# A float32 two-block network on one core: high and low parts of the feed-forward input side by side, as one moving operand of 512 columns

## What is computed

```
def swiglu(x, w1, w2):
    gu = x @ w1
    g, u = gu[..., :D_FF], gu[..., D_FF:]
    return (jax.nn.silu(g) * u) @ w2

for l in range(DEPTH):                                    # block 1, DEPTH = 2
    x = x + 0.5 * swiglu(rms_norm(x, ffn1_norm[l]), ffn1_w1[l], ffn1_w2[l])
    x = x + hybrid_mixer(rms_norm(x, mix_norm[l]), ...)
    x = x + 0.5 * swiglu(rms_norm(x, ffn2_norm[l]), ffn2_w1[l], ffn2_w2[l])
return rms_norm(x, final_norm)
```

## Time and profile before

| what | value |
|---|---|
| median of 3 runs | 2327.35 us (2321.9 to 2327.54) |
| profiled execution | 2319.62 us |
| its span, first to last instruction | 2317.8 us |
| mean granted TensorE clock in it | 0.931 of full |
| busy share of the span | TensorE 88%, its weight loads 84%, VectorE 64%, ScalarE 50%, GpSimd 6% |
| matmuls | 15496, each with a weight load |
| read from HBM | 327.27 MB |

### The profile page before, as it was taken

One profiled execution on the slowest core, in us unless ns is written; L12 is line 12 of the kernel. 1 busy time (PEld: TensorE's weight loads), 2 busy tenths in 40 slices (PEclk: granted clock), 3 DMA queues, 4 the chain that ended last, 5 costly groups with the idle time before them and its releaser, 6 DMA issues.

```text
span 2317.8 us, 40039 instructions
## 1 busy us (share of the span) xinstructions
PE 2045.6 (88%) x15496; PEld 1951.3 (84%) x15496; DVE 1472.7 (64%) x2084; ACT 1168.3 (50%) x1804; POOL 149.5 (6%) x167
## 2 busy tenths in 40 slices
PE   6999877879999999878879998787899978887998
PEld 6999867879999999867879998665799976667998
DVE  5665698655655655698656655564598465626963
ACT  5445644444444445644444445554565445536753
POOL 0071000000000001000000001000300000003000
PEclk9999989989999999989989999887899988878999
DMA  5545323345545545323345454331254532202543
GB/s 206 182 167 184 128 100 109 118 165 173 178 163 191 184 162 184 128 100 110 123 161 180 170 170 156 109 109 37 73 197 157 190 125 98 103 19 106 210 147 118
DMA packets 53535, 329.83 MB, mean 142 GB/s; under 512 B 5936, under 2 KB 6704, under 8 KB 27952
## 3 DMA queue, kind: packets, MB, share of 16 engines
q1 hardware_dynamic: 53424, 328.34, 41.0%
HBM read 327.27 MB, written 1.05 MB: 142 GB/s over the span
## 4 chain that ended last, share of the span: by engine, by line
PE 49%; DVE 16%; ACT 12%; issue 10%; DVEq 7%; DMA 3%; POOLq 3%; POOL 1%; ACTq 0%; SPq 0%
PE bank L605 13%; PE bank L606 13%; PE bank L607 13%; DVE w_lo L584 7%; ACT w_hi L578 5%; DMA raw<-in_w 2%; DVEq L915 2%; DVE conv L1239 2%; DVEq L1233 2%; PE bank L617 1%; ACT probs L924 1%; PE bank L626 1%; PE bank L619 1%; PE bank L1522 1%; PE bank L1538 1%
## 5 line engine op out<-in xcount | busy, mean ns | idle before, releaser
L584 DVE TENSOR_TENSOR w_lo<-raw,w_hi 128x2048 fp32r<-128x2048 f32 (+3 forms) x358 | 719.2, 2010 | 433.1 <-ACT w_hi L578 430.6
L605 PE MATMUL bank<-h_hi,w_hi 128*128 128x256 f32 x2704 | 784.9, 290 | 17.7 <-DVE w_lo L584 16.4
L606 PE MATMUL bank<-h_lo,w_hi 128*128 128x256 f32 x2704 | 775.7, 287 | 0.0
L607 PE MATMUL bank<-h_hi,w_lo 128*128 128x256 f32 x2704 | 774.9, 287 | 0.0
L578 ACT ACTIVATE w_hi<-raw 128x2048 fp32r<-128x2048 f32 (+3 forms) x358 | 600.9, 1680 | 170.7 <-DMA raw<-in_w 118.3
L605 PEld LDWEIGHTS bank<-h_hi,w_hi 128*128 128x128 f32 x2704 | 531.2, 196 | 23.2 <-DVE w_lo L584 17.5
L606 PEld LDWEIGHTS bank<-h_lo,w_hi 128*128 128x128 f32 x2704 | 531.0, 196 | 1.0
L607 PEld LDWEIGHTS bank<-h_hi,w_lo 128*128 128x128 f32 x2704 | 529.9, 196 | 0.0
L605 PE MATMUL bank<-hid_hi,w_hi 128*128 128x256 f32 x1056 | 296.2, 281 | 6.5 <-DVE conv L1879 6.5
L606 PE MATMUL bank<-hid_lo,w_hi 128*128 128x256 f32 x1056 | 296.2, 280 | 0.0
L607 PE MATMUL bank<-hid_hi,w_lo 128*128 128x256 f32 x1056 | 296.1, 280 | 0.0
(11 more groups left out here) (356 smaller groups left out, 3275.2 us busy)
## 6 DMA issues: line engine op xcount, KB each, us to landing
raw<-in_w SPq DMA_DIRECT2D x198, 1024.0 KB, 4.8
raw<-in_w SPq DMA_DIRECT2D x96, 704.0 KB, 4.0
raw<-in_w SPq DMA_DIRECT2D x52, 768.0 KB, 4.2
raw<-in_w SPq DMA_DIRECT2D x8, 512.0 KB, 3.5
raw<-in_w SPq DMA_DIRECT2D x4, 576.0 KB, 3.9
x<-in_x SPq DMA_DIRECT2D x1, 1024.0 KB, 4.7
out<-x SPq DMA_DIRECT2D x4, 256.0 KB, 2.4
const<-in_const SPq DMA_DIRECT2D x1, 548.0 KB, 5.2
```

The costliest lines, as they stand in the source:

```text
L584: dve.tensor_tensor(w_lo[:, s % SPLIT_SLOTS, 0:n], raw[:, s % RAW_SLOTS, 0:n], w_hi[:, s % SPLIT_SLOTS, 0:n].bitcast(F32), ALU.subtract).t ...
L605: pe.matmul(out, hi, x_hi, start=start, stop=False)
L606: pe.matmul(out, hi, x_lo, start=False, stop=False)
L607: return pe.matmul(out, lo, x_hi, start=False, stop=stop)
```

## The change

In block 1's feed-forwards, from up unit 4 on and in all down tiles, the high and the low part of the activation become one moving operand of 512 columns. They now lie side by side for each tile (`h_pair`, `hid_pair`; the old names are views of them). The high weights stream both parts in one matmul: high x high lands in columns 0 to 255 of a bank, high weight x low activation in columns 256 to 511. The low weights still stream the high part alone, into columns 0 to 255. A product is then two matmuls instead of three, and its result is the sum of the two halves of a bank.

An up unit therefore takes two banks, one for the gate and one for the linear columns: banks 4 and 5 or 6 and 7 by the parity of j. TensorE waits for the release of unit j-2 instead of j-4. The halves are added when PSUM is emptied: ScalarE copies the second half of each bank to SBUF (`joint`, two tiles of `scr`), VectorE adds the first halves to it in two instructions, drains, and scales the sum. For a down tile VectorE adds the second half to x, drains, and adds the first. Units 0 to 3, the mixers and block 2 keep three matmuls for a product.

```
+PAIRS_FROM = 4
@@ Groups
             if kind.startswith("up"):
                 main, bank = i % 4, i % 4
+                if pairs and i >= PAIRS_FROM:
+                    bank = 4 + 2 * (i % 2)
@@ build
-        h_hi = sbuf("h_hi", [P, KT, T], F32R)
-        h_lo = sbuf("h_lo", [P, KT, T], F32R)
+        h_pair = sbuf("h_pair", [P, KT, 2, T], F32R)
+        h_hi, h_lo = h_pair[:, :, 0], h_pair[:, :, 1]
+        joint = scr[:, 4:8].rearrange("p (a b) t -> p a (b t)", a=2)
-            hid_hi = sbuf("hid_hi", [P, FT, T], F32R, phase)
-            hid_lo = sbuf("hid_lo", [P, FT, T], F32R, phase)
+            hid_pair = sbuf("hid_pair", [P, FT, 2, T], F32R, phase)
+            hid_hi, hid_lo = hid_pair[:, :, 0], hid_pair[:, :, 1]
+        def pair_product(pe, bank, s, block, pair, start, stop):
+            hi = w_hi[:, s % SPLIT_SLOTS, block * P:block * P + P]
+            lo = w_lo[:, s % SPLIT_SLOTS, block * P:block * P + P]
+            pe.matmul(bank[:, 0:2 * T], hi, pair.rearrange("p a t -> p (a t)"), start=start, stop=False)
+            return pe.matmul(bank[:, 0:T], lo, pair[:, 0], start=False, stop=stop)
@@ ffn_pe
+            def paired_unit(j, more):
+                s = at + j
+                weights_ready(pe, s, more)
+                for half in range(2):
+                    for k in range(KT):
+                        last = pair_product(pe, banks[4 + 2 * (j % 2) + half], s, half * KT + k, h_pair[:, k], k == 0, k == KT - 1)
+                last.then_inc(work.done_sem.sem, 1)
...
+                work.wait_banks_free(pe, l, [(up, 4), (up, 5)])
+                with pe.Fori(0, 4) as it:
+                    for u in range(4, 8):
+                        pe.wait_ge(*work.taken(l, (up, 0), it * 4 + (u - 2)))
+                        paired_unit(u, it * 4)
...
+                            if paired:
+                                last = pair_product(pe, banks[2 + g], s, b, hid_pair[:, k], k == 0, k == FT - 1)
@@ ffn_act, gated
+                if j >= PAIRS_FROM:
+                    act.wait_ge(*work.done(l, (up, 0), more + j))
+                    for half in range(2):
+                        last = act.activation(joint[:, parity, half * T:half * T + T], banks[4 + 2 * parity + half][:, T:2 * T], ACT.Copy)
+                    last.then_inc(second_out.sem, 1)
@@ ffn_dve, gated
+                else:
+                    dve.wait_ge(*second_out(l, more + (w * (FT - PAIRS_FROM) + j + 1 - PAIRS_FROM)))
+                    for half in range(2):
+                        part = joint[:, parity, half * T:half * T + T]
+                        dve.tensor_tensor(part, part, banks[4 + 2 * parity + half][:, 0:T], ALU.add)
+                    dve.drain()
+                    dve.tensor_tensor(halves(scaled[:, parity]), halves(joint[:, parity]), by_r(2),
+                                      ALU.mult).then_inc(work.freed["v"].sem, 1)
@@ ffn_dve, residual
                 dve.wait_ge(*work.done(l, (down, 0), more * 2 + 2 * t))
+                dve.scalar_tensor_tensor(x[:, more + t], banks[2 + t % 2][:, T:2 * T], 0.5, x[:, more + t], ALU.mult, ALU.add)
+                dve.drain()
                 dve.scalar_tensor_tensor(x[:, more + t], banks[2 + t % 2][:, 0:T], 0.5, x[:, more + t], ALU.mult,
                                          ALU.add).then_inc(work.freed["v"].sem, 1)
```

More of the change, by code:

```diff
@@ L153, in __init__ @@
             self.mark[g], self.bank[g] = marks, bank
-            self.before[g] = last.get(bank)
+            taken = (bank, bank + 1) if pairs and kind.startswith("up") and i >= PAIRS_FROM else (bank,)
+            self.before[g] = [(b, last.get(b)) for b in taken]
             if who is None:
@@ L158, in __init__ @@
             self.freer[g] = (who, self.freed_until[who])
-            last[bank] = g
+            for b in taken:
+                last[b] = g
         self.marks, self.last = marks, last
@@ L418, in bank_free @@
             def bank_free(self, layer, group):
[L420 removed]
+                (bank, before), = self.g.before[group]
                 wrapped = before is None
[L422 to L423 removed]
+                who, n = self.g.freer[before or self.g.last[bank]]
                 s = self.freed[who]
@@ L433, in wait_banks_free @@
                     latest[who] = max(latest.get(who, n), n)
-                for group in groups:
-                    before = self.g.before[group]
+                for bank, before in (b for group in groups for b in self.g.before[group]):
                     wrapped = before is None
-                    who, n = self.g.freer[before or self.g.last[self.g.bank[group]]]
+                    who, n = self.g.freer[before or self.g.last[bank]]
                     latest[who] = max(latest.get(who, -10 ** 9), n - (self.freed[who].per if wrapped else 0))
@@ L763, in ffn_pe @@
                 by_tiles(pe, work, l, [((up, 3), at + 3)], lambda k: nm.true_ready(l, k + 1))
+                first = 4
+            else:
+                first_products(pe, nm, work, l, m, [((up, j), at + j) for j in range(2)], lambda: norm_pe(pe, work, nm, l, n))
+                first = 2
+            if paired:
+                for j in range(first, 4):
+                    up_unit(j, 0)
+                work.wait_banks_free(pe, l, [(up, 4), (up, 5)])
[3 more added lines that the diff above has]
+                        paired_unit(u, it * 4)
+                for j in range(20, FT):
+                    pe.wait_ge(*work.taken(l, (up, j - 2)))
+                    paired_unit(j, 0)
+            else:
+                for j in range(first, 4):
+                    up_unit(j, 0)
                 with pe.Fori(0, 4) as it:
@@ L770, in ffn_pe @@
                     up_unit(j, 0)
-            else:
-                first_products(pe, nm, work, l, m, [((up, j), at + j) for j in range(2)], lambda: norm_pe(pe, work, nm, l, n))
-                with pe.Fori(0, 5) as it:
-                    for u in range(4):
-                        pe.wait_ge(*work.taken(l, (up, 0), it * 4 + (2 + u - 4)))
-                        up_unit(2 + u, it * 4)
             with pe.Fori(0, KT // 2) as it:
@@ L789, in ffn_pe @@
                                 pe.wait_ge(*hidden(l, w * FT + k + 1))
-                            last = product(pe, banks[2 + g][:, 0:T], s, b, hid_hi[:, k], hid_lo[:, k],
-                                           k == 0, k == FT - 1)
+                            if paired:
+                                last = pair_product(pe, banks[2 + g], s, b, hid_pair[:, k], k == 0, k == FT - 1)
+                            else:
+                                last = product(pe, banks[2 + g][:, 0:T], s, b, hid_hi[:, k], hid_lo[:, k],
+                                               k == 0, k == FT - 1)
                         last.then_inc(work.done_sem.sem, 1)
@@ L802, in gated @@
                 act.activation(hid_hi[:, more + j], hid[:, parity], ACT.Copy).then_inc(hid_hi_ready.sem, 1)
+            for j in range(4):
+                gated(j, 0, j % 2, lambda: split.until(at + j + FFN_AHEAD))
             with act.Fori(0, 4) as it:
-                for u in range(4):
+                for u in range(4, 8):
                     gated(u, it * 4, u % 2, lambda: split_hi(act, at + u + FFN_AHEAD, it * 4, it * 2))
-            split.next = at + 16 + FFN_AHEAD
-            for j in range(16, FT):
+            split.next = at + 20 + FFN_AHEAD
+            for j in range(20, FT):
                 gated(j, 0, j % 2, lambda: split.until(at + j + FFN_AHEAD))
@@ L849, in ffn_dve @@
             dve.wait_ge(*n1.std_ready(l, n + 1))
-            for j in range(2):
+            for j in range(4):
                 gated(j, 0, j % 2, lambda: split.until(at + j + FFN_AHEAD), j > 0)
             with dve.Fori(0, 4) as it:
-                for u in range(2, 6):
+                for u in range(4, 8):
                     gated(u, it * 4, u % 2, lambda: split_lo(dve, at + u + FFN_AHEAD, it * 4))
-            split.next = at + 18 + FFN_AHEAD
-            for j in range(18, FT):
+            split.next = at + 20 + FFN_AHEAD
+            for j in range(20, FT):
                 gated(j, 0, j % 2, lambda: split.until(at + j + FFN_AHEAD))
```

18 lines of the change are left out of this document (9 added, 9 removed).

## The result

Median 2351.83 us (2344.5 to 2356.79, 4 runs) against 2324.62 for the kernel before beside it: ratio 1.0112, 95% interval [1.0093, 1.0131]. The change costs 1.1%, some 27 us. The forecast, 2331 with a range up to 2348, was too low. The profiled execution after took 2347.02 us, span 2345.2 against 2317.8. TensorE issues 13640 matmuls instead of 15496, the 1856 fewer that the diff promises, so the work it was meant to save is gone and the time is longer.

A forecast was written before the change was run, and what follows sets the result against it. TensorE bounds the kernel before; after, the ring does in the up phase, cancelling TensorE's saving there. Later x, 2 x 1.0 + 2 x 0.5 = 3.0, 3.5 us with semaphore delays, on 2327.35 gives 2331, range 2318 to 2348.

The forecast's parts named there:

- What bounds before: Up units before the change: TensorE's pace, 5.76 us a unit, sets the limit; VectorE has about 0.5 us spare.
- the ring: Up units: scaling, silu, w_hi, w_lo wait on each other across VectorE and ScalarE; 5.19 us a unit, 6.04 after.
- rival C: Up units: ScalarE's copies leave their cover under w_lo and lengthen the ring; 2351 us, chance 0.20.
- rival B: TensorE stays the limit because additions overlap more or the late start hides them; 2308 us, or 2312; chance 0.13.
- TensorE's paired unit: Up product 0.3475 us instead of 0.360, unit 5.56 instead of 5.76; down product 0.345 instead of 0.3525.
- From unit 18 ... the ring falls to 4.86: Late up units: 1408-wide splits shorten the ring to 4.86 us, under TensorE; last scaling 118.8 us after the first.
- A buffer turns in 7.2 us against TensorE's 7.59, so by unit 36 most is regained: Down tiles: the late weight stream catches up with TensorE; unit 36 at 160.2 us against 159.7 before.
- My sum: Feed-forward ends: +1.0 us each for second and fourth, +0.5 for first and third; 3.0, with semaphore delays 3.5.
- The restart behind the last x: Third feed-forward's first matmul waits for x, 2.54 us idle before; x about 1.0 us later, TensorE's last matmul 0.3 earlier.
- Rival D: TensorE's clock falls because it idles 0.48 us of 6.04 in ten up units a feed-forward; 2348 us, chance 0.04.
- The second addition at the end: Last down tile: its second addition into x costs 0.34 + 0.09 = 0.43 us more.

The follow-up runs named there:

- e2: Changed kernel with ScalarE's w_hi split placed ahead of the silu instead of behind it: 2323.34 us, ratio 1.0008 to the kernel before.
- e7: Changed kernel without the two additions and the drain of a paired up unit: 2332.98 us, ratio 1.0017 to the kernel before.
- e9: Changed kernel, down products unpaired, split loops ending at unit 15, w_hi before silu, positions loaded first, last x addition before last w_lo: 2313.12 us, ratio 0.9954.
- e1: Changed kernel with both up-unit loops ending at unit 15 instead of 19, so units 22 and 23 split at 1408 columns: 2349.36 us, ratio 1.0103.
- e5: Changed kernel with the down tiles' weight loads halved in block 1's feed-forwards: 2343.49 us, ratio 1.0053 to the kernel before.
- e6: Kernel before the change with the down tiles' weight loads halved in the same way: 2327.42 us, ratio 0.9995.
- e4: Changed kernel with only the down products paired, up units as before the change: 2332.18 us, ratio 1.0032 to the kernel before.
- e10: Kernel before, no pairing, with w_hi before silu, positions loaded first, last x addition before last w_lo: 2319.81 us, ratio 0.9982.

## Why the prediction was wrong

**What bounds before: right.** TensorE, with about half a microsecond of room in the ring.

**The ring: right.** 6.04 us forecast, 6.01 measured; additions and drain 0.82 against 0.85; the scaling 0.69, not dearer. The copies keep their cover, so rival C's price came true, 2351, by none of its mechanism. e2 and e7 open the ring from two sides and the up phase falls back to TensorE's pace in both. VectorE's idle third did not help (rival B): it was a wait inside the ring, and the ring kept it.

**TensorE's paired unit: half right.** Down 0.346 us a product against 0.345. Up 0.354 against 0.3475, so 2.0 us saved a feed-forward by 18 units instead of 3.6. This changed nothing here, since the ring is longer, but it is all that the pairing can win in e9.

**"From unit 18 ... the ring falls to 4.86": the first failed step.** Two errors. I read the width of a split from the weight unit's own size, and did not follow the diff into the loops, whose width is fixed at 2048 up to unit 19: 2.4 us (e1). And I let units 19 to 21 finish at TensorE's pace, 118.8 for the last scaling, where the ring's own sum says 106.15 + 3 x 4.86 = 120.7; e1 measured 120.3. A ring that is behind must be counted to its end. With 0.4 off for a ring of 6.01 instead of 6.04, that is 2.4 + 1.9 - 0.4 = 3.9 us, from 118.8 to the measured 122.7.

**"A buffer turns in 7.2 us against TensorE's 7.59, so by unit 36 most is regained": the second failed step.** The five turns from unit 26 to unit 36 were 7.34, 8.69, 7.41, 7.23 and 7.45 us (the starts 670.63 to 708.75), the long one with a wait of 2.17 us for its transfer. Their mean is 7.62, just TensorE's 22 x 0.346 = 7.61, so the margin was gone and next to nothing was regained. Unit 26 was split 126.2 us after the first scaling (forecast 124.0, before 120.9) and unit 36 at 164.3 (forecast 160.2, before 159.6): of the 4.1 us by which the forecast missed, 2.2 came from the late entry and 1.9 from the turns. At the last scaling the second feed-forward was 5.5 us late, at its last x 5.0. In the fourth the mean turn was 7.46, and a wait of 3.73 us for one transfer (unit 38, at 1426.46) took back what that had regained. e5 returns 1.9 to 4.0 us of the loss, e6 0.1 to 1.1. My sum had +1.0 for the second and the fourth feed-forward and +0.5 for the first and the third; the last three measured +5.0, +6.8 and +5.6. Nor did TensorE's last matmul come 0.3 us earlier, as I had it, but 2.0 later, since the ring had held TensorE too.

**The first feed-forward: not in the prediction.** I had no term for SyncE's queue, in which the positions stand behind loads that wait for the delayed up units. The GpSimd wait of 3.47 us was already in the trace of before. It grew to 7.66, and the first feed-forward lost 9.7. The late positions are only a part of it. In e2 and e7 the other feed-forwards are nearly those of before and the positions arrive as early as before (125.4 and 126.7, before 126.35), yet GpSimd's chain lasts 50 and 52 us instead of 47, the square waits 6.67 and 8.58, and the first feed-forward ends late (+183.9, +188.2). What makes the same GpSimd instructions longer stays open. With the positions first the chain is out of the way whatever it lasts, and e9 has +177.1.

**The restart behind the last x: only its sign was right.** TensorE's idle time at the third feed-forward's start grew by 3.0 us instead of by 1.3, and the clock behind it fell from 0.89 to 0.77. Rival D did not happen inside the up phase: the clock stayed 1.00 there (60 to 150 us), with waits of up to 0.4 us for the scaling. The Trainium skill (TensorE: Matmul & The Clock Gate, "A second HAM failure mode: psum-queue depth-cycling") tells of a clock that goes up and down where TensorE idles shortly between groups on cycling banks; the 1.00 of the windows above does not show that here.

**The second addition at the end: right in size** (0.49 us from the first to the second, against 0.43); e4's +0.4 to +1.5 us a feed-forward are more than it explains.

What stays open: the 3 us that e5 is still behind; 2.6 us in the mixer between the third and the fourth feed-forward (320.3 us from last x to first scaling, before 317.7); and, since e9 makes its edits together, how much each of the three orders brings with the pairing. e10 gives their sum without it: 2.4 us a feed-forward at the mark, 9.6 in all, while the last x of its fourth feed-forward stands 6.0 us earlier in the execution than before (1403.4 against 1409.4). The last x ahead of the last w_lo, alone in the kernel after, was not run.

## What to carry to other kernels

When an engine with idle time to spare shows a wait in every round, look for the ring through the queues of two engines: once that ring is longer than the bounding engine's unit, time added to any link of it is paid in full, and a swap of two independent instructions can open it (e2: ratio 1.0008 instead of 1.0112). When an early phase comes late, ask of each later phase by how much it is faster than its slowest supply, transfers with their scatter included; a forecast margin of 0.4 us in 7.6 turned out to be none. And a saving on the bounding engine shows at the end only when the last consumer stands behind nothing else in its queue: in e2, with the last x behind a w_lo, little or nothing of the pairing's saving arrived; in e9, with it ahead, 1.7 to 1.9 us a feed-forward. The version to keep is e9, 0.46% faster than the kernel before, with only the up products paired.

## What the runs showed of the hardware

- A matmul of 512 moving columns beside one of 256: together 0.354 us with the up units' tiles and 0.346 with the down tiles', against 0.360 and 0.3525 for three of 256. Joining two saves 2% of the time of a product, not the 3.5% that the row of 512-column matmuls alone suggests for the up units.
- Block 2 is the same code in all kernels, and the time from the fourth feed-forward's last x to the end of the span was 905 to 924 us over the traces of the 14 kernels (908.4 before, 905.0 after). Marks inside the program told differences of 1 us where the whole time could not.
